# Context's keys, values and queries moved between the first block's stages, and two norms taken together

## The reference, cut to what matters

```
mod = silu(c) @ ada_w[l] + ada_b[l]                  # 9 vectors of 1024 a layer
h = modulate(rms_norm(x, norm_ffn1[l]), sh1, sc1)
x = x + 0.5 * g1 * swiglu(h, ffn1_w_in[l], ffn1_w_out[l])
h = modulate(rms_norm(x, norm_mix[l]), sh2, sc2)
x = x + g2 * token_mix(h, ...)
h = modulate(rms_norm(x, norm_ffn2[l]), sh3, sc3)
x = x + 0.5 * g3 * swiglu(h, ffn2_w_in[l], ffn2_w_out[l])
...
return rms_norm(x, final_norm)
```

```
mx = split(silu(c) @ ada_w[i] + ada_b[i]);  mc = split(silu(c_ctx) @ ada_w[i] + ada_b[i])
h_x = modulate(rms_norm(x, g[0]), mx[0], mx[1])
h_c = modulate(rms_norm(ctx, g[0]), mc[0], mc[1])
q_x, k_x, v_x = rope(h_x @ w_q), rope(h_x @ w_k), h_x @ w_v
q_c, k_c, v_c = h_c @ w_q, h_c @ w_k, h_c @ w_v
```

## Time and profile before

| | us |
|---|---|
| median of 3 runs | 2368.6 |
| lowest and highest | 2367.8, 2374.0 |
| profiled execution, its own time | 2363.91 |
| its span in the trace | 2361.7 |
| PE busy | 2124.7 (90%) |
| DVE busy | 1677.8 (71%) |
| ACT busy | 972.4 (41%) |

### The profile page before, as it was taken

The page is one execution under the profiler, slowest core; times in us unless marked ns, Lnnn a source line. Parts: engine busy times, 40 slices in busy tenths (PEclk is TensorE's granted clock), DMA queues, the critical chain, the costliest instruction groups (busy, mean ns, idle before and its releaser), DMA issues.

```text
span 2361.7 us, 34275 instructions
## 1 busy us (share of the span) xinstructions
PE 2124.7 (90%) x14517; PEld 1919.8 (81%) x14517; DVE 1677.8 (71%) x2345; ACT 972.4 (41%) x1276; POOL 28.3 (1%) x33
## 2 busy tenths in 40 slices
PE   3899989999899989999979699799999888668998
PEld 3899888899899987899957477588888676558998
DVE  7777677777777758789975474866656567877754
ACT  3333434433443344433342463432222347665443
POOL 0000000000000000000000000000000001010000
PEclk8899999999999999999989799899999999879999
DMA  8678544688688754578733003244434232125751
GB/s 302 225 265 285 187 127 157 211 269 282 223 266 275 242 163 143 168 254 273 251 124 128 14 1 125 71 143 143 143 125 162 88 125 65 45 69 184 255 188 52
DMA packets 328161, 402.66 MB, mean 170 GB/s; under 512 B 9051, under 2 KB 256841, under 8 KB 328009
## 3 DMA queue, kind: packets, MB, share of 16 engines
q1 hardware_dynamic: 324608, 396.11, 50.8%
q10 hardware_dynamic: 3400, 4.38, 0.6%
HBM read 399.41 MB, written 1.05 MB: 170 GB/s over the span
## 4 chain that ended last, share of the span: by engine, by line
PE 45%; DVE 9%; ACT 4%; issue 2%; DVEq 0%; ACTq 0%
PE pb L533 44%; DVE ACC L1561 1%; DVE wl L1553 1%; DVE RS L1640 1%; ACT L_y L1099 1%; DVE Y L1561 1%; PE pb L969 1%; DVE T L1561 1%; DVE XC L1553 1%; ACT wh L1098 0%; ACT L1099 0%; DVE SM L2059 0%; ACT A_P L1433 0%; DVE L_u L1561 0%; ACT L_x L1099 0%
## 5 line engine op out<-in xcount | busy, mean ns | idle before, releaser
L533 PE MATMUL pb<-Hh,wh 128*128 128x256 f32 (+1 forms) x2464 | 765.5, 311 | 62.2 <-DVE Hl L1561 43.8
L533 PE MATMUL pb<-Hl,wh 128*128 128x256 f32 (+1 forms) x2464 | 758.4, 308 | 0.0
L533 PE MATMUL pb<-Hh,wl 128*128 128x256 f32 (+1 forms) x2464 | 757.4, 307 | 0.0
L1553 DVE TENSOR_TENSOR wl<-raw,wh 128x2048 fp32r<-128x2048 f32 (+3 forms) x265 | 587.6, 2220 | 224.2 <-ACT wh L1098 223.9
L1098 ACT ACTIVATE wh<-raw 128x2048 fp32r<-128x2048 f32 (+3 forms) x265 | 490.4, 1852 | 277.3 <-PE pb L533 235.6
L533 PEld LDWEIGHTS pb<-Hh,wh 128*128 128x128 f32 x2464 | 479.6, 195 | 88.3 <-issue 54.3
L533 PEld LDWEIGHTS pb<-Hl,wh 128*128 128x128 f32 x2464 | 479.7, 195 | 19.9 <-issue 1.2
L533 PEld LDWEIGHTS pb<-Hh,wl 128*128 128x128 f32 x2464 | 479.5, 195 | 19.3
L533 PE MATMUL pb<-Bh,wh 128*128 128x256 f32 (+1 forms) x1344 | 412.8, 307 | 9.7 <-DVE Y L1553 4.4
L533 PE MATMUL pb<-Bl,wh 128*128 128x256 f32 (+1 forms) x1344 | 407.5, 303 | 0.0
L533 PE MATMUL pb<-Bh,wl 128*128 128x256 f32 (+1 forms) x1344 | 407.5, 303 | 0.0
(11 more groups left out here) (232 smaller groups left out, 2024.3 us busy)
## 6 DMA issues: line engine op xcount, KB each, us to landing
raw<-in_ada_w_dram SPq DMA_DIRECT2D x120, 1024.0 KB, 5.6
raw<-in_ffn_w_in_dram SPq DMA_DIRECT2D x88, 1024.0 KB, 5.8
raw<-in_mlp_w_dram SPq DMA_DIRECT2D x64, 1024.0 KB, 5.5
raw<-in_ffn_w_out_dram SPq DMA_DIRECT2D x32, 1024.0 KB, 5.7
raw<-in_mix_w_in_dram SPq DMA_DIRECT2D x22, 1024.0 KB, 5.5
raw<-in_ffn_w_out_dram SPq DMA_DIRECT2D x16, 768.0 KB, 4.6
raw<-in_lru_w_in_dram SPq DMA_DIRECT2D x10, 1024.0 KB, 5.4
raw<-in_mix_w_out_dram SPq DMA_DIRECT2D x8, 1024.0 KB, 5.3
```

Source lines behind the costliest of these rows:

```text
L533: return e.matmul(o, l, r, start=st, stop=sp, skip_group_check=True)
L1553: return e.tensor_tensor(o, a, b, f)
```

## The change

It plans six more units of the attention's weights for the context alone: k2c before layer 0's second FFN, v2c before layer 1's first, q2c before layer 1's mix, q2c before its second FFN, and two q2c at the entry. `cx_open` does half of such a unit behind the first pair of the hand-over's sums, `cx_half` the other half behind the last. k2, v2, q2 then run over x alone. The context's norm is done inside layer 0's first FFN: squares, sums and small steps of DVE and ACT (`c_high`, `c_low`, `C_STEPS`). At the entry, the sums of x² and of (final gain times x)² are made together in layer 1's last FFN. With r² the mean of the first plus eps, the second norm's root mean square follows from the second sum and r², so that one root and one reciprocal serve h; the scaling of XC by the final norm comes later. The split that belonged to the last fo or mo of a stage goes to `late`, and `catch_up` does it: on ACT before `modulated`, on DVE behind it. The ada loads are spread by their due places (`ends`, `rate`) rather than evenly. The first two sorts of context vectors are loaded apart from x's, 8 loads more, with the passes 152 as before. `A_kr`, `A_v` and the rotations of q2 change their shapes. The program's DMA scratch is 1024.

```diff
 LO_STEPS = [(0, 0), (1, 0), (2, 0), (0, 1), (1, 1), (2, 1), (3, 0), (3, 1)]
-LAST = 0.92
-ROOM = {"iq": 0.0, "ik": 0.0, "u": 0.0, "q": 0.0, "k": 0.0, "va": 0.0, "v": 0.0, "lr": 0.0, "lw": 0.0, "lo": 0.0, "lg": 0.5}
+ROOM = {"iq": 0.0, "ik": 0.0, "u": 0.0, "q": 0.0, "k": 0.0, "va": 0.0, "v": 0.0, "o2": 0.0, "lr": 0.0, "lw": 0.0, "lo": 0.0, "lg": 0.5}
...
+    w2 = t["attn_w_qkv_2"][0]
+    ahead = [("k2c", 1024), ("v2c", 1280), ("q2c", 0), ("q2c", 256), ("q2c", 512), ("q2c", 768)]
+
+    def context():
+        cols(w2, *ahead.pop(0))
 
...
         for f, (wi, wo, seg) in enumerate((("ffn1_w_in", "ffn1_w_out", 0), ("ffn2_w_in", "ffn2_w_out", 6))):
             if f:
                 need((0, l, 3), (0, l, 4))
+                if l:
+                    context()
...
                     cols(t["mix_w_out"][l], "mo", 256 * j)
             need((0, l, seg), (0, l, seg + 1))
+            if f or l:
+                context()
...
                 if kind == "in":
+                    if not f and not l and (c, j) == (2, 0):
+                        need((1, 0, 0, 2), (1, 0, 1, 2))
                     cols(wi, "g", (4 * c + j) * 256)
                     cols(wi, "gu", FF + (4 * c + j) * 256)
...
-    w = t["attn_w_qkv_2"][0]
+    need((1, 0, 0, 1), (1, 0, 1, 1))
+    context()
+    context()
+    w = w2
     for key, c0 in (("k2", 1024), ("v2", 1280), ("q2", 0), ("q2", 256), ("q2", 512), ("q2", 768)):
...
             src = w[512 * (i % 2):512 * (i % 2) + 512, s * 1024 + (i // 2) * 512:s * 1024 + (i // 2) * 512 + 512]
             adas.append((seg, i, vecs, due[seg], src))
...
-    room = np.cumsum([ROOM.get(u[0], 1.0) for u in units])
+
+    room = np.concatenate([[0.0], np.cumsum([ROOM.get(u[0], 1.0) for u in units])])
+    cost = np.cumsum([len(a[2]) for a in adas])
+    ends = {}
+    for a, c in zip(adas, cost):
+        ends[a[3]] = c
+    stream, ai, budget, sent = [], 0, 0.0, 0
     for i, u in enumerate(units):
-        want = first + (len(adas) - first) * room[i] / (LAST * room[-1])
-        while ai < len(adas) and (ai < want or adas[ai][3] <= i):
+        rate = max([(c - budget) / max(room[d] - room[i], 0.1) for d, c in ends.items() if d > i] + [0.0])
+        budget = max(budget + max(rate, 0.0) * (room[i + 1] - room[i]), ends.get(i, 0))
+        while ai < len(adas) and (cost[ai] <= budget + 1e-6 or adas[ai][3] <= i):
             stream.append(("a", adas[ai]))
             ai += 1
...
+
+            def cx_open():
+
+                key = CX[cxs[0]]
+                cxs[0] += 1
+                E.wait_ge("c.h", 8)
+                u = (key, weights(key), fill("cx"))
+                cx_half(u, 0)
+                return u
+
+            def cx_half(u, m):
+                key, (vh, vl, nk, ncol), p = u
+                c = slice(128 * m, 128 * m + 128)
+                x = slice(256 + 128 * m, 384 + 128 * m)
+                for kt in range(8):
+                    if key == "v2c":
+                        l, r = (Hh[:, kt, x], Hl[:, kt, x]), (vh[:, kt, :], vl[:, kt, :])
+                    else:
+                        l, r = (vh[:, kt, c], vl[:, kt, c]), (Hh[:, kt, 256:512], Hl[:, kt, 256:512])
+                    ins = mm3(p[:, 256 * m:256 * m + 256], l, r, kt == 0, kt == 7)
+                if m:
+                    full(ins, "cx")
+                    spent()
+
             def ffn(l, seg, sums, first=None):
+                between = cx_open() if seg or l else None
                 mods((0, 0, l, seg), (0, 0, l, seg + 1))
                 sums.add()
+                if between:
+                    cx_half(between, 1)
...
                 for kind, c, j in mlp_steps(FFN_PAIRS):
                     b = c % 2
                     if kind == "in":
+                        if first and (c, j) == (0, 3):
+                            csum = Sums(256)
+                            for kt in range(8):
+                                E.wait_ge("sq", E.up("sq"))
+                                mm(csum.p[:, 0:256], ONES, c_slot(kt), kt == 0, kt == 7).then_inc(sems["sq.read"], 1)
+                        if first and (c, j) == (2, 0):
+                            mods((1, 2, 0, 0), (1, 2, 0, 1))
                         fm("g", "g", h_at, 256, need, fresh=c == 0 and j == 0)
...
                     if c == last:
-                        sums = Sums(256)
+                        sums = Sums(512 if l and seg else 256)
                     for m in range(4):
...
             def mix(l, sums):
+                between = cx_open() if l else None
                 mods((0, 0, l, 3), (0, 0, l, 4))
                 sums.add()
+                if between:
+                    cx_half(between, 1)
                 need = h_need()
                 h0 = E.n["h"] - 8
...
-            mods((1, 1, 0, 0), (1, 1, 0, 1), (1, 2, 0, 0), (1, 2, 0, 1))
+            between = cx_open()
+            mods((1, 1, 0, 0), (1, 1, 0, 1))
             sums.add()
-            need = h_need(512)
+            SQUARES["first"] = E.n["sq"]
+            cx_half(between, 1)
+            cx_half(cx_open(), 1)
+            need = h_need()
             h0 = E.n["h"] - 8
-            fm("k2", "k2", h_at, 512, need, fresh=True)
-            tm("v2", "v2", 4, h0)
+            fm("k2", "k2", h_at, 256, need, fresh=True)
+            tm("v2", "v2", 2, h0)
             k2_0 = E.n["k2.read"]
...
-                E.up("q2.ctx", 2)
+                fm("q2", "q2", h_at, 256, need, said="q2.read")
                 if j:
-                    turn2(2 * j - 2)
-                    turn2(2 * j - 1)
+                    turn2(j - 1)
             mods((1, 1, 0, 2), (1, 2, 0, 2))
...
+
+            def cx():
+
+                k = cxs[0]
+                cxs[0] += 1
+                ahead(CX[k])
+                act(CX_TO[k][:, :, :], full("cx")[:, :].rearrange("p (m n) -> p m n", m=2), ACT.Copy).then_inc(sems["cx.read"], 1)
+
...
+                        if c == last and m == 3:
+                            late.append("fo")
+                        else:
+                            ahead("fo")
                         E.up("x", 2)
...
                 root_mean(256)
+                catch_up()
                 modulated([(0, shift(0, 0, l, 3))])
+                if l:
+                    cx()
                 E.wait_ge("h", E.n["h"])
...
             e.dma_start(A_KM[:, :], t["kconst"][:, K_R2:K_R2 + 640]).then_inc(sems["l_a"], 16)
             e.dma_start(A_snk[:, 0:16], t["attn_sink_2"][0:1, :].to_broadcast([128, 16])).then_inc(sems["l_a"], 16)
-            root_mean(512)
-            modulated([(0, shift(1, 1, 0, 0)), (256, shift(1, 2, 0, 0))])
+            E.wait_ge("rs.w", 1)
+            act(RS[:, 0:256], RS[:, 0:256], ACT.Sqrt).then_inc(sems["rs.sqrt"], 1)
+            act(RS[:, 256:512], PB[SUMS_BANK][:, 0:256], ACT.Sqrt, bias=EPSC, scale=1.0 / D).then_inc(sems["rs.sqrt"], 1)
+            catch_up()
+            modulated([(0, shift(1, 1, 0, 0))])
+            cx()
+            cx()
...
+
+            late = []
+
+            def catch_up():
+                while late:
+                    ahead(late.pop())
+
+            cxs = [0]
+
+            def cx():
+
+                cxs[0] += 1
+                ahead(CX[cxs[0] - 1])
...
                 modulated([(0, S_GAIN, shift(0, 0, l, seg))])
+                catch_up()
+                if seg or l:
+                    cx()
                 last, gate = len(FFN_PAIRS) - 1, False
...
+                        if c == last and m == 3:
+                            late.append("fo")
+                        else:
+                            ahead("fo")
                         p = full("fo")
...
             gain(S_GX, 1, 1, 0, 0, ng(0, 0))
-            gain(S_GC, 1, 2, 0, 0, ng(0, 0))
-            mean_root(512)
-            modulated([(0, S_GX, shift(1, 1, 0, 0)), (256, S_GC, shift(1, 2, 0, 0))])
+            own()
+            E.step(tt(S_GX, S_GX, vt("n_fin"), ALU.mult))
+            E.wait_ge("sq.read", SQUARES["first"])
+            E.step(ts(RS[:, 0:256], PB[SUMS_BANK][:, 0:256], EPS / D, EPS * EPS, ALU.mult, ALU.add))
+            own()
+            stt(RS[:, 0:256], PB[SUMS_BANK][:, 256:512], 1.0 / D, RS[:, 0:256], ALU.mult, ALU.add).then_inc(sems["rs.w"], 1)
+            mean_root(256)
+            modulated([(0, S_GX, shift(1, 1, 0, 0))])
+            catch_up()
+            cx()
+            cx()
+            ahead("k2")
+            ahead("v2")
+            E.wait_ge("rs.sqrt", E.up("rs.sqrt"))
+            E.step(e.reciprocal(RS[:, 256:512], RS[:, 256:512]))
+            own()
+            for kt in range(8):
+                E.step(stt(XC[:, kt, 0:256], XC[:, kt, 0:256], vt("n_fin", kt, 1), RS[:, 256:512], ALU.mult, ALU.mult))
```

More of the change, by code:

```diff
@@ L224, in build @@
     for seg in sorted(due, key=lambda s: (due[s], s)):
-        b, l, s = seg
+        b, l, s, *only = seg
         w = t["ada_w_2" if b else "ada_w"][l]
-        vecs = [0] if b == 0 else ([1, 2] if l == 0 or s < 2 else [1])
```

(54 more changed lines are left out.)

123 lines of the change are left out of this document (69 added, 54 removed), and 4 rows, old and new, of tables (GROUPS, RING).

## The result

| | before | after |
|---|---|---|
| median of 6 runs | 2366.8 | 2380.5 |
| lowest and highest | 2362.7, 2374.0 | 2379.7, 2384.8 |
| span of the profiled execution | 2361.7 | 2378.7 |

The changed kernel is slower: its time is 1.0059 of the kernel before, 95% interval 1.0042 to 1.0076, 13.7 us by the medians and 17.0 by the two profiled spans.

A forecast was written before the change was run, and what follows sets the result against it. It took TensorE, busy 90%, to bound the kernel. Hand-overs +43.5, entry −30.2 and the rest +0.5 gave +13.8: 2377.7 for the profiled execution, 2382.4 on the median, range 2358 to 2396.

The forecast's parts named there:

- The four hand-overs: Stage changes with a context unit: PE waits some 11 us for weights split behind the norm; +9.9, +10.3, +9.1, +14.2.
- the third term: FFN to mix in layer 1: no ada pass before the first weights, unit ends later than now, +9.1 us.
- Rival B: The gaps are really filled, first weights ready with the first Hl: −30 us, 2339; chance 10%.
- The slow stretch: PE at half clock after idling at a stage change, costing some 1.9 us each; forecast to stay.
- the 43.5: Sum in us of the losses forecast at the four stage changes that get a context unit.
- the lower bound: If first weights cost PE nothing, each stage-change loss is smaller by about 10 us, the four about nothing.
- The entry: Second block's start up to the attention's first matmul: 81.4 us instead of 113.3, −31.9; −30.2 with +1.7 before it.
- the wide sums: Before the entry, four of the last fo's eight sums over 512 columns instead of 256: 0.43 more each, +1.7 us.
- The first FFN: Layer 0's first FFN: context's eight sums +3.4 us; added DVE work, still not over PE, +1 (0 to 10).
- rival D: Layer 0's first FFN can't be fed in units 10 to 30: +10 on top, 2392; chance 14%.
- The attention: Second block's attention: queries half as wide before its steps, −1.5 us (−3 to 0).
- Before the last MLP: Seven ACC steps standing before the last MLP's weights are gone: −1.6 us (−3 to 0).

The follow-up runs named there:

- a_nolate: The changed kernel with the last fo's and last mo's split back in its old place, without late and catch_up: 2351.8 us, 0.992 of the kernel before.
- b_late: The kernel before with only the change's late and catch_up added, no context unit between stages: 2357.6 us, ratio 0.9948.
- b_rate: The kernel before with only the change's new spreading of the ada loads: 2370.8 us, ratio 1.0004 to the kernel before.

## Why the prediction was right, and which terms were off

**The four hand-overs: right, with their mechanism.** From F to the first weight matmul the forecast had 18.8, 16.0 and 21.3 at the last three; the trace has 18.9, 15.8 and 20.6. For the first it gives only that the unit ends 9.9 later; it starts at F+20.3 and ends 10.4 later. In the sum of the third term 0.2 was lost: F+16.0, 5.76 and 1.9 make F+23.7, not F+23.5. Rival B, filled gaps, would have needed the first split ahead of the norm; a_nolate makes it so, and the time goes below the kernel before. `late` alone gains too (b_late), so the loss is of the two together. The slow stretch behind the wait was there too: 0.50 in 442 to 447.

**What the 43.5 is worth as a price is less sure.** It was read as a loss that would vanish with its cause. Taking the cause away gave 28.7 (the four stages alone 30.0). The step that failed is the lower bound "each term is the smaller by about 10": the wait also gave DVE time for work that otherwise stands behind it, and the clock falls a unit later instead. Rival B's 2339 was for this reason too low; a_nolate is that rival, at 2352.

**The entry: −31.9 forecast from F, −28.1 measured.** The first keys were due at F+45.6 and came at F+45.0 (1288.6). The second q2c started at F+18.3 (forecast 18.7), and PE stood 5.3 us before the keys (forecast about 7). The miss lies behind: from there to the attention 40.3 instead of 35.8. PE's clock was at half over the four k/kr groups, which came 3.5 us apart instead of 2.2; four times 1.3 is about the 4.5 that are missing:

```profile
1289.00:1294.00 5.00, 4.39 (x10) 3.04 (x11) 2.52 (x6) 0.90 (x2) 0.00 (x0) 0.50 0.01 2
1294.00:1299.00 5.00, 4.43 (x12) 3.08 (x11) 1.78 (x4) 1.75 (x4) 0.00 (x0) 0.50 0.00 0
```

I had put the slow stretch behind the four waits and forgotten it behind the fifth.

**A term left out: flushes move with the passes.** Columns of ACC are flushed by PE, 8 records and 0.94 us each. Of PE's matmuls from ACC alone, in layer 0's first FFN, its second, and layer 1's second, before and then after (length, busy time, PEclk, DMA share, GB/s):

```profile
54.31:270.60 216.29, 6.62 (x56) 0.96 0.76 252
415.09:625.42 210.33, 7.46 (x64) 0.98 0.77 253
975.22:1192.46 217.24, 17.14 (x144) 0.98 0.73 245
```

```profile
52.57:276.85 224.28, 11.35 (x96) 0.96 0.85 284
422.04:647.04 225.00, 12.10 (x104) 0.97 0.81 275
1017.20:1243.58 226.38, 11.35 (x96) 0.97 0.66 217
```

+4.7, +4.6 and −5.8 us; layer 1's first FFN has 72 records before and 96 after, +2.8. That is why three of the FFNs lost more and layer 1's last less than the sum had. With the flushes taken out, the four stages lost 10.1, 10.1, 7.4 and 14.9; the terms are 9.9, 10.3, 9.1 and 14.2, and the last stage also holds the 1.7 of the wide sums. In layer 1's mix the first unit ends 9.6 later, near the term, and the rest of the stage is 2 us shorter; why is open. All flushes together are 608 records in both kernels, so the forecast of the total did not suffer, but each stage's did.

**The first FFN: +4.4 forecast with csum and DVE, +8.0 measured.** 4.7 is flushes, 3.4 the sums as forecast. Windows of the whole stage and of about its units 10 to 30 (PE, PEld, DVE, ACT, POOL busy, PEclk, DMA share, GB/s):

```profile
52.57:276.85 224.28, 213.82 (x1728) 212.39 (x1729) 194.25 (x255) 90.79 (x89) 0.00 (x0) 0.96 0.85 284
115.00:235.00 120.00, 120.00 (x1008) 120.00 (x1007) 108.07 (x128) 48.42 (x40) 0.00 (x0) 1.00 0.93 316
```

DVE was busy 194 of 224 us. PE waited for a split once, 1.7 near the end (0.7 before); two waits near the start, 3.4 and 5.4, are in the kernel before too (4.6 and 5.4). So rival D did not come: in the units where it was due PE never stood, at 316 GB/s where the forecast had 340.

**The attention: −1.5 forecast, −7.2 measured.** 5.5 of it are in the steps, 1.7 are two flushes fewer behind them. The term was sized at 1.5 with no working shown. Undoing the narrow splits gives back 3.8 of the 5.5, in one execution of a stretch that varies by some 5 us.

**Before the last MLP: −1.6 forecast, a small loss measured.** The seven ACC steps are gone from there, but PE's two waits at that place are 4.1 and 4.2 us as before, so the steps had not been on its path. From the sums before the recurrence to the last MLP's first matmul the changed kernel takes 2.6 more; b_rate has 2.4 more as well, so it belongs to the new spreading.

These misses nearly cancel. Against the forecast's terms the entry has 3.8 more, the first FFN 3.6, the part behind the attention 2.8 and the start 1.1; the attention has 5.7 less, layer 0's mix 1.3 and the four hand-overs with the wide sums 1.1. So the total is closer than the terms deserve, and that is luck: 17.0 in the spans against 13.8. The medians come closer still, 13.7 against the same 13.8, only because the profiled execution of the kernel before was 2.9 below its median.

## What to carry to other kernels

Work placed into a gap shifts every "so many units ahead" by one: ask what the split or load that used to be for the second unit now stands for. Two edits that each gain can lose together (0.8% and 0.5% faster here, 0.6% slower as a pair), so cost the pair in the queue's order, on the engine that both use. When a wait is taken away, count what the waiting engines did for others meanwhile, because that part comes back as the next wait.
